# Expert weights in a two-block decoder kernel: three loops over the rounds, whole transfers in the middle one

## The reference, cut to what matters

```python
weights = p_grp * top_p / jnp.sum(top_p, axis=-1, keepdims=True)
experts = grp[:, None] * EXPERTS_PER_GROUP + top_i.astype(jnp.int32)
...
def run_block(args):
    tok, e = args
    xb = xf[tok]
    hid = jax.nn.silu(xb @ w_gate[e]) * (xb @ w_up[e])
    return hid @ w_down[e]
...
x = x + gt2 * hierarchical_moe(h2, ...)
return rms_norm(x, g_final)
```

## Time and profile before

| | before |
|---|---|
| median of 3 runs | 946.2 us (943.51 to 946.67) |
| profiled execution | 941.32 us |
| its span in the trace | 939.6 us |
| TensorE busy | 786.0 us, 84% |
| DVE, ACT busy | 471.9 us, 338.1 us |
| mean granted clock of TensorE | 0.941 |
| DMA | 278.78 MB, mean 297 GB/s |

### The profile page before, as it was taken

One profiled execution on the slowest core, in us unless ns is written; L12 is line 12 of the kernel. 1 busy time (PEld: TensorE's weight loads), 2 busy tenths in 40 slices (PEclk: granted clock), 3 DMA queues, 4 the chain that ended last, 5 costly groups with the idle time before them and its releaser, 6 DMA issues.

```text
span 939.6 us, 20123 instructions
## 1 busy us (share of the span) xinstructions
PE 786.0 (84%) x7481; PEld 600.4 (64%) x7482; DVE 471.9 (50%) x818; ACT 338.1 (36%) x509; POOL 54.8 (6%) x145
## 2 busy tenths in 40 slices
PE   8999999899999999999999997975575566776554
PEld 7999789678888887979989754543232333343222
DVE  4664787757786853776895633341221212232123
ACT  7443666453543436655873411211010101010112
POOL 4000000000000000020130000000000000000000
PEclk9999999999999999999999998998887979898797
DMA  7876332648989745562447979999999999999995
GB/s 236 290 277 220 111 107 75 224 147 317 342 298 333 264 151 205 160 216 91 136 152 284 424 270 420 420 422 421 422 423 421 423 420 422 423 421 423 421 423 214
DMA packets 97523, 278.78 MB, mean 297 GB/s; under 512 B 9375, under 2 KB 69194, under 8 KB 80074
## 3 DMA queue, kind: packets, MB, share of 16 engines
q1 hardware_dynamic: 97194, 277.95, 77.2%
q10 hardware_dynamic: 288, 0.27, 0.1%
HBM read 277.15 MB, written 1.05 MB: 296 GB/s over the span
## 4 chain that ended last, share of the span: by engine, by line
PE 57%; DMA 14%; SPq 12%; DVE 8%; ACT 5%; issue 4%; DVEq 0%; ACTq 0%; POOL 0%; POOLq 0%
SPq L861 10%; PE bank L2170 8%; DMA Whi<-in_w_up 6%; PE bank L385 5%; PE bank L387 5%; PE bank L386 5%; PE bank L2192 4%; PE bank L1808 4%; PE bank L1810 4%; PE bank L1809 4%; DMA projR<-in_w_up 3%; DMA Wlo<-in_w_up 3%; DMA Wlo<-in_w_gate_up 2%; DVE Whi_r L327 1%; PE acc L1834 1%
## 5 line engine op out<-in xcount | busy, mean ns | idle before, releaser
L385 PE MATMUL bank<-R_r,Whi_r 128*128 128x256 f32 x448 | 128.9, 288 | 3.0 <-DVE Whi_r L2233 2.6
L386 PE MATMUL bank<-R_r,Whi_r 128*128 128x256 f32 x448 | 126.9, 283 | 0.0
L3023 DVE TENSOR_TENSOR V<-V,bank 64x256 f32<-64x256 f32 x34 | 14.4, 424 | 216.0 <-ACT V L1530 216.0
L387 PE MATMUL bank<-R_r,Whi_r 128*128 128x256 f32 x368 | 104.3, 283 | 0.0
L385 PEld LDWEIGHTS bank<-R_r,Whi_r 128*128 128x128 f32 x448 | 86.0, 192 | 6.4 <-DVE Whi_r L2233 3.2
L1530 ACT ACTIVATE V<-bank 64x256 f32<-64x256 f32 x34 | 12.8, 375 | 204.7 <-PE bank L2170 204.7
L386 PEld LDWEIGHTS bank<-R_r,Whi_r 128*128 128x128 f32 x448 | 86.0, 192 | 0.1
L2170 PE MATMUL bank<-Whi,S 128*32 128x256 f32 x832 | 59.4, 450 | 30.9 <-DMA Whi<-in_w_up 30.6
L318 ACT ACTIVATE Whi_r<-Wlo 128x1024 fp32r<-128x1024 f32 x62 | 62.1, 1051 | 56.2 <-PE bank L387 53.7
L2170 PE MATMUL bank<-w_gate,S 128*32 128x256 f32 x352 | 52.2, 461 | 33.9 <-DMA projR<-in_w_up 33.9
L327 DVE TENSOR_TENSOR Whi_r<-Wlo,Whi_r 128x1024 fp32r<-128x1024 f32 x48 | 58.0, 1250 | 31.6 <-ACT Whi_r L318 31.6
(11 more groups left out here) (520 smaller groups left out, 1601.3 us busy)
## 6 DMA issues: line engine op xcount, KB each, us to landing
Wlo<-in_w_down SPq DMA_DIRECT2D x29, 1024.0 KB, 20.4
Wlo<-in_w_in SPq DMA_DIRECT2D x24, 1024.0 KB, 5.3
Wlo<-in_w_gate_up SPq DMA_DIRECT2D x22, 1024.0 KB, 7.7
Whi<-in_w_down SPq DMA_DIRECT2D x20, 1024.0 KB, 25.3
R<-in_w_down SPq DMA_DIRECT2D x18, 1024.0 KB, 25.4
Wlo<-in_w_ada SPq DMA_DIRECT2D x14, 1024.0 KB, 9.1
Whi<-in_w_gate SPq DMA_DIRECT2D x10, 1280.0 KB, 24.2
Whi<-in_w_up SPq DMA_DIRECT2D x10, 1280.0 KB, 26.9
```

What stands on the lines that cost most here:

```text
L385: pe.matmul(o, w_hi[:, c], tile(x_hi, k), start=start, stop=False, skip_group_check=True)
L386: pe.matmul(o, w_hi[:, c], tile(x_lo, k), start=False, stop=False, skip_group_check=True)
L387: return pe.matmul(o, w_lo[:, c], tile(x_hi, k), start=False, stop=(k == KT - 1), skip_group_check=True)
```

## The change

The loop over rounds becomes three on SP and on TensorE: rounds 0 and 1 (SP: round 1), rounds 2 to 7, and rounds 8 to 10, as `WHOLE = (2, 8)` has it. `part` is 0, 1 or 2.

- Part 0 is as before: pieces, and SP waits for `gu_half` before the first pieces.
- Part 1: SP waits for `gu_done`, then loads gate whole and up whole (2048 KB each), then after `yw_done` the down matrix in one transfer. TensorE waits for both matrices before its first product, and for the whole down matrix before its down product.
- Part 2: SP waits for `gu_done`, loads gate whole, up in its two pieces, and the down matrix in two. TensorE waits for the gate matrix, then runs eight products of 128 x 128 by 256 of ones into a half of bank 2 that nothing reads, then waits for the first piece of up, and at k = 5 for the second.

The semaphores of the pieces are renamed: `gu0`, `gu1`, `gu2` and `wd0`, `wd1` for each set instead of `gu_full{par}_{h}` and `wd_full{par}_{h}`, with counts that follow from the part. `fin_rinv` and `y_ready` of the final norm move onto DVE's shared semaphore. DVE, ACT and POOL keep one loop each.

```diff
+                           ("perm_set", 2), ("fin_copy", 1), ("fin_sq", 2), ("fin_bias", 1), ("fin_mul", 4),
+                           ("fin_rinv", 1), ("y_ready", 2))),
...
+        WHOLE = (2, 8)
...
-            def expert_part(name, e, par, halves=(0, 1)):
+            def expert_part(name, e, par, piece, full):
...
+                if name == "wd":
+                    rows, n = w.rearrange("a (h p c) n -> p (a h) (c n)", h=2, c=2), 2
+                    if piece is not None:
+                        rows, n = rows[:, piece:piece + 1, :], 1
+                        place = place[:, piece * 2 * D:(piece + 1) * 2 * D]
+                else:
+                    rows, n = w.rearrange("a (p k) n -> p a (k n)", p=P), 1
+                    if piece is not None:
+                        c = slice(piece * 5 * DE, (5, KT)[piece] * DE)
+                        rows, place = rows[:, :, c], place[:, c]
+                sp.dma_start(place.rearrange("p (a n) -> p a n", a=n), rows
+                             ).then_inc(sem(f"{full}_full{par}"), 16)
...
-                    for h in range(2):
-                        sp.wait_ge(*upto("gu_done" if h else "gu_half", used))
-                        expert_part("wg", number, par, (h,))
-                        expert_part("wu", number, par, (h,))
+                    if part == 0:
+                        for h in range(2):
+                            sp.wait_ge(*upto("gu_done" if h else "gu_half", used))
+                            expert_pieces("wg", number, par, (h,))
+                            expert_pieces("wu", number, par, (h,))
+                    else:
+                        sp.wait_ge(*upto("gu_done", used))
+                        expert_part("wg", number, par, None, "gu0")
+                        if part == 1:
+                            expert_part("wu", number, par, None, "gu1")
+                        else:
+                            expert_part("wu", number, par, 0, "gu1")
+                            expert_part("wu", number, par, 1, "gu2")
                     sp.wait_ge(*upto("yw_done", used))
-                    expert_part("wd", number, par)
+                    if part == 1:
+                        expert_part("wd", number, par, None, "wd0")
+                    else:
+                        expert_pieces("wd", number, par)
...
+            with sp.Fori(1, WHOLE[0]) as i:
+                expert(i, 0, 0)
+            with sp.Fori(*WHOLE) as i:
+                expert(i, 0, 1)
+            with sp.Fori(WHOLE[1], NO // NBUF) as i:
+                expert(i, 0, 2)
...
+                def gu_full(h):
+                    at = i * 32 + 32 if part == 0 else i * 16 + 16 * (WHOLE[0] + 1)
+                    if h == 2:
+                        at = i * 16 - 16 * (WHOLE[1] - 1)
+                    return sem(f"gu{h}_full{par}"), at
...
-                            pe.wait_ge(*upto(f"gu_full{par}_0", i * 32 + 32))
+                            pe.wait_ge(*gu_full(0))
+                            if part == 2:
+                                for _ in range(8):
+                                    pe.matmul(bank[2][:, T:2 * T], ones[:, 0:P], ones[:, :],
+                                              start=True, stop=True)
+                            if part:
+                                pe.wait_ge(*gu_full(1))
...
-                                if w is None:
-                                    pe.wait_ge(*upto(f"gu_full{par}_1", i * 32 + 32))
+                                if w is None and part != 1:
+                                    pe.wait_ge(*gu_full(2 if part else 1))
...
-                            if f % 2 == 0:
-                                pe.wait_ge(*upto(f"wd_full{par}_{f // 2}", i * 16 + 16))
+                            if f == 0 or f == 2 and part != 1:
+                                pe.wait_ge(*wd_full(f // 2))
```

More of the change, by code:

```diff
@@ L847, in _ @@
             sp_rest(sp, wout2)
-            def expert_part(name, e, par, halves=(0, 1)):
+            def expert_part(name, e, par, piece, full):
                 at, w = {"wg": (0, "w_gate_2"), "wu": (1, "w_up_2"), "wd": (2, "w_down_2")}[name]
                 w = d[w][0][bass.ds(e, 1)]
[L853 to L861, removed]
+                place = Wx[par][at]
+                if name == "wd":
[10 more added lines that the diff above has]
+                             ).then_inc(sem(f"{full}_full{par}"), 16)
@@ L863, in _, with expert_pieces @@
+            def expert_pieces(name, e, par, pieces=(0, 1)):
+                for h in pieces:
+                    expert_part(name, e, par, h, ("wd", "gu")[name != "wd"] + str(h))
             for j in range(2):
                 sp.wait_ge(*upto(f"proj2_done{j}", IN2_FULL // 512))
-            expert_part("wg", 0, 0)
-            expert_part("wg", 1, 1)
+            expert_pieces("wg", 0, 0)
+            expert_pieces("wg", 1, 1)
             sp.wait_ge(*upto("mix2_ready", 3))
-            expert_part("wu", 2, 2)
+            expert_pieces("wu", 2, 2)
@@ L869, in _ @@
             for j in range(2):
                 sp.wait_ge(*upto(f"wout2_done{j}", 2))
[L871 to L872 removed]
+            expert_pieces("wu", 0, 0)
+            expert_pieces("wd", 0, 0)
             sp.wait_ge(*upto("pp_done", 2))
[L874 to L875 removed]
+            expert_pieces("wu", 1, 1)
+            expert_pieces("wd", 1, 1)
             sp.wait_ge(*upto("og_rows"))
@@ L880, in _, with expert @@
             sp.wait_ge(*upto("xtok_done", 4))
-            expert_part("wg", 2, 2)
+            expert_pieces("wg", 2, 2)
             sp.wait_ge(*upto("xs_done", KT))
-            expert_part("wd", 2, 2)
+            expert_pieces("wd", 2, 2)
             sp.wait_ge(*upto("tbl_ready"))
-            def expert(i, par):
+            def expert(i, par, part):
                 windows = sp.value_load(tbl[0:1, bass.ds(i * NBUF + (NW_AT + par), 1)],
@@ L894, in expert @@
                                          min_val=0, max_val=MAXWIN)
-                    for h in range(2):
-                        sp.wait_ge(*upto("gu_done" if h else "gu_half", used))
-                        expert_part("wg", number, par, (h,))
-                        expert_part("wu", number, par, (h,))
+                    if part == 0:
[11 more added lines that the diff above has]
+                            expert_part("wu", number, par, 1, "gu2")
                     sp.wait_ge(*upto("yw_done", used))
-                    expert_part("wd", number, par)
+                    if part == 1:
+                        expert_part("wd", number, par, None, "wd0")
+                    else:
+                        expert_pieces("wd", number, par)
                     if par < NBUF - 1:
-                        expert(i, par + 1)
-            with sp.Fori(1, NO // NBUF) as i:
-                expert(i, 0)
+                        expert(i, par + 1, part)
+            with sp.Fori(1, WHOLE[0]) as i:
[4 more added lines that the diff above has]
+                expert(i, 0, 2)
             for t in range(TT):
@@ L2147, in _, with expert, wd_full @@
             pe_now, pe_seen = expert_registers(pe)
-            def expert(i, par):
+            def expert(i, par, part):
                 gate, up, down = Wx[par]
+                def gu_full(h):
[3 more added lines that the diff above has]
+                    return sem(f"gu{h}_full{par}"), at
+                def wd_full(h):
+                    return sem(f"wd{h}_full{par}"), i * 16 + 16 - 16 * (WHOLE[1] - WHOLE[0]) * (h and part == 2)
                 windows = pe.snap(pe_now, min_val=0, max_val=NWIN)
@@ L2209, in expert @@
                     if par < NBUF - 1:
-                        expert(i, par + 1)
-            with pe.Fori(0, NO // NBUF) as i:
-                expert(i, 0)
+                        expert(i, par + 1, part)
+            with pe.Fori(0, WHOLE[0]) as i:
+                expert(i, 0, 0)
+            with pe.Fori(*WHOLE) as i:
+                expert(i, 0, 1)
+            with pe.Fori(WHOLE[1], NO // NBUF) as i:
+                expert(i, 0, 2)
             total = pe.snap(pe_seen, min_val=1, max_val=MAXWIN)
```

1 line of the change is left out of this document (removed).

## The result

The changed kernel takes 946.31 us (median of 22 runs, 944.21 to 948.26), the kernel before 944.99 (22 runs). The ratio, taken over runs of both kernels, is 1.0019, interval 1.0010 to 1.0028: slower by 1.8 us (the medians by themselves differ by 1.3), clear of noise and less than the 0.3% that the prediction called a difference. The forecast was 943.4, faster by 2.8. The time lies in the stated range, the sign is wrong.

A forecast was written before the change was run, and what follows sets the result against it. The saturated DMA weight stream, about 422 GB/s, was taken to bound the expert phase. Stream -4.0 and tail +1.2 gave -2.8 us: 941.3 to 938.5 profiled, 943.4 as median, with a range of 939.5 to 948.8.

The forecast's parts named there:

- in rounds 8 and 9 before the last expert they hide in TensorE's waits: TensorE's eight dummy products per expert, 3.5 us warm or 6.9 cold, were to cost nothing before the last expert.
- The stream's gain: Weight stream: fewer packets at 14 ns each bring the last landing 4.0 us earlier, 3.6 from rounds 2 to 7.
- the line for a 16 KB packet: Weight queue: straight line of packet time over size, 36.8 ns per KB plus 14 ns, giving about 0.62 us.
- Three copies of the code: Loop code of TensorE and SP, there three times: fetches cost 0, or 2 us if all came on the path.
- The tail: Last expert on TensorE: down ends 2.8 us behind sight of the last down piece, 1.2 us worse than before.
- The half clock that I had counted inside the last expert: TensorE's last expert: 3.4 us of half clock inside the work, adding 1.7 us to the tail.
- The middle: Middle rounds: SP's and TensorE's later starts, up to 2.3 and 3.7 us, are covered and cost nothing.
- The thin place of round 2: Round 2's first loads, at 590.73 us: 6 us of stream cover, so issuing 1 us later is covered.
- packets that move worse: Rival "slower": 16 KB packets move worse than 10 and 6 KB ones; at 3% some 952.8 us; chance of slower 0.17.
- the tail eats the gain: Rival in the last expert: 6.8 us of half clock behind the dummies, +2.9 against -4.0, 945.1 us; chance 0.12.
- down before L + 1.5: Sign of being wrong: the last down product ends under 1.5 us after L, when TensorE sees the last down piece.

The follow-up runs named there:

- b_copies: The kernel before, same transfers and computation, with the loops of SP and TensorE written out three times; ratio 1.0007 to the kernel before.
- mid_only: Against the kernel before: whole transfers in rounds 2 to 7 only, pieces and no dummy products in later rounds; ratio 0.9986 to the kernel before.
- a_nodummy: The changed kernel without the eight dummy products of rounds 8 and 9; ratio 0.9991 to the kernel before.
- a_shift6: The changed kernel with the third loop two rounds earlier, WHOLE = (2, 6); ratio 0.9994 to the kernel before.

## Why the prediction was wrong

Two steps failed, and both hid work in TensorE's waits without adding it up: "in rounds 8 and 9 before the last expert they hide in TensorE's waits" (the dummies), and "the first pass over each copy falls where the engine waits anyway [...] 0" (the code). Its sum, with what the runs gave:

- **The stream's gain, -4.0 us: mis-sized.** The mechanism was right and so was the line for a 16 KB packet (615 ns). The price of a packet was 9.5 ns and not 14 (the prediction's line leaves 13 by its own numbers: 390 - 10.24 x 36.8). I took busy time per packet, but the busy shares are above 1.00, so packets of one engine overlap; that only part of a packet's own time is time of the stream fits this, and no run tests it. By periods the 18 experts gave 18 x 0.15 = 2.7 and the last four 0.3; b_copies to mid_only, the same code and fetches, is -3.0.
- **Three copies of the code, 0: failed.** That the first pass falls where the engine waits holds for TensorE as long as it waits (mid_only), and not for the stream, whose engines carry the fetches: +1.7 us (b_copies). With both the last landing came 1.2 us earlier, not 4.0. I had put 2 us on it as the far end and given it no weight, though the 1.1 us of a fetch was in my hands.
- **The tail, +1.2 us: failed, and by the most.** I started the last expert's chain at the landing of the gate matrix, L - 9.9. In after it starts at 923.86, L - 5.7, because TensorE is not idle before it. The hiding was said without adding up an expert: 3.7 of dummies, 3.7 of product, 2.0 ahead of down and 1.9 of down are 11.3 us of 14.9 warm, and a stall of 2 to 3 us with the half clock behind it, 1.2 to 2.9, makes 15.6 to 16.7. The tail grew by 4.0 us. Taken apart: without the dummies it is 4.2 us (a_nodummy), with the first pass two rounds earlier 1.9 (a_shift6), without the dummies and with the gate in pieces 1.5, though the first pass stays in round 8 (mid_only); 2.1 is that of before. The half clock that I had counted inside the last expert did not come: its dummies, product and down are warm.
- **The middle, 0: right.** No stage is without work, though SP waits for the end of the product. The thin place of round 2 held: the stream has no gap there.

-3.0 of packets, +1.7 of code, +4.0 of tail: +2.7 from P, against +1.8 timed. Of the two failed steps the tail weighs more: with its +4.0 and no cost of the code the sum would still be +1.0; with the code's +1.7 and the forecast's tail of +1.2 it would be -0.1. The terms are taken from one execution of each kernel.

That the time lies inside the range is no merit of the mechanism: the range was wide enough for packets that move worse, which did not happen. The rival nearest to the result was "the tail eats the gain", 945.1, by another cause (cold clock alone), and too small. The chance of 0.17 for slower went to packets that move worse "or by a stall that no row shows"; stalls came, but the rival had neither a place nor a price for them. Of the three signs of being wrong that the prediction named (a period not shorter, a stage under 415 GB/s, down before L + 1.5) none came; what gave it away was down at L + 5.6, outside the forecast 2 to 3 us.

## What to carry to other kernels

When a loop is split to treat some rounds apart, count its code: where the DMA engines are the bound, each fetch of new code is taken from the stream (0.9 to 1.2 us a copy here), and the engine that executes it stands still for it (2 to 3 us here). Where that engine has no wait left to take this up, the first pass should not fall into the last rounds. Work put into an engine's idle time (warming products here) must be added up over a whole period with its stalls and its clock, not only at the one place where it is wanted. Busy time per packet overstated a packet's price here, where the shares are above 1 (14 ns for 9.5); a period or a cut twice as fine gave it.

## What the runs showed that I had not expected

- With gate and up sent to 64 of 128 partitions at a time, one half after the other, the same packets move at 234 GB/s instead of 422, all 16 engines busy, and the 8 KB packets of the down matrix between them are slow too. The Trainium skill, "DMA: Bandwidth & Descriptors", section "Rules for kernel authors", advises one transfer to 128 partitions over two to disjoint halves and says that the halves share the same engines and serialize. This case agrees with the advice (1.35 times the kernel's time); that halves take turns on engines which are busy in either case does not by itself explain a loss of 45%, and no run here separates the cause.
- Where TensorE has no other wait, a stall of 2 to 3 us for code is followed by half clock, so that it costs 1.2 to 1.7 us more in the 32 instructions behind it (3.1 to 3.6 against 1.9 us).
- On a saturated stream the 16 engines finish a transfer 2.1 us apart even without fetches (first and last completion of the last transfer in before), and a landing is that of the last engine.
